# Building the expert gates inside the expert blocks: three PEER passes of a two-model forward on one core

## The chip, the cores and the metric

One core of a Trainium2 chip runs the whole program in one launch. The metric is the time of one execution in microseconds (us); lower is better.

## The reference, cut to what matters

A first block of mixers and a convolutional FFN is followed by two layers (l = 0, 1). Each layer ends in a PEER stage: every token picks, for each of 8 heads, 16 of 128 x 128 = 16384 experts, by the sums of two key scores, and the chosen experts act as a one-hidden-layer network.

```python
q      = rmsnorm(x) @ wq                    # [T, 8 heads x 128]
s1, s2 = q_half1 @ keys1.T, q_half2 @ keys2.T        # 128 scores each, per head
best 16 of (top16(s1)[:,None] + top16(s2)[None,:])   # row key, column key, softmax weight w
h      = gelu(x @ U[expert])                # for the chosen experts only
y      = sum over the chosen: w * h * V[expert]
```

The kernel computes it densely. It takes x @ U for all 16384 experts, multiplies by a gate that is zero wherever an expert was not chosen, and multiplies by all of V. The gate of a token is the 128 x 128 matrix sum_i w_i onehot(row_i) onehot(col_i)^T over its 128 chosen pairs, a matmul with the choice index on the contraction axis. There are T = 256 tokens a stream. Layer 0 does it for two streams (s = 0 and 1), layer 1 for one (s = 1): three passes.

## The kernel before, in words

Weights stream from HBM through `ring`, NS = 4 slots of 128 x 1024 float32 (512 KB). SyncE issues all their DMAs in one fixed order (`order`, function `stream`, L242): the transfer into a slot waits until the block that used the slot before is done (`blocks_done`). A product is made in three float32r parts: ScalarE writes the rounded high part into `ring_hi` (NH = 3 slots), another engine writes block minus high part over the ring slot (`ring_lo`), and TensorE multiplies hi x hi, hi x lo and lo x hi.

A PEER pass before the change, by lines:

- norm of the streams (`rms_phase`, L352 to L411), then queries in plain float32 (`product`, L1617) for both streams at once, evacuated by ScalarE (L1624), with a phase of their own;
- U (L1649 to L1861): TensorE first makes the key scores (L1691, all token tiles of both streams in pass one), ScalarE makes the high part of x (L1739), GpSimd its low part (L1667). Then 128 blocks c: ScalarE high part (L1745), GpSimd low part (L1673), TensorE 24 matmuls of 256 columns (L1706 to L1708) into banks 4 to 7, ScalarE gelu into S[:, c, :] (L1750). Beside it VectorE does the routing of 4 (pass one), 0 (pass two) or 2 tiles (pass three) (L1806 to L1859), and TensorE transposes its result (L1716);
- gate (L1871 to L1957), a phase of its own: 64 groups of 4 tokens. The one-hot columns come from GpSimd (L1885, 4 a group), the weighted one-hot rows half from VectorE (L1921), half from ScalarE (L1897, L1902). TensorE does 4 float32 matmuls of 128 columns a group (L1949; each has two rows in the trace), VectorE multiplies the bank into S (L1927);
- V (L1964 to L2040): 128 blocks. ScalarE high part of V (L1979); VectorE high and low part of the gate weights S[:, c, :] (L2001, L2003) and low part of V (L1994); TensorE 12 matmuls of 512 columns (L2027 to L2031) into banks 0 to 3;
- y is copied, transposed and added to X (L2053 to L2070).

Every phase ends in a barrier of all engines (L339). Loops are `Fori` of 12 blocks; within an engine the order is the written one, and every wait stands in that order.

Of the kernel before, what the change touches and what calls it, by code (L numbers as in the profile page):

```python
# [8 lines left out]
F32 = mybir.dt.float32  # L9
# [12 lines left out]
NS = 4  # L22
# [15 lines left out]
def small_columns():  # L38
# [123 lines left out]
def build(nc, x, smalls, consts, mix_tables, tables, axial, w_in1, w_lru, w_br, w_o1, w_f1, w_f2, ada, w_in2,  # L162
          w_out2, w_q2, keys2, peer_u, peer_v, out):
    ctx = ExitStack()
    with ctx:
# [12 lines left out]
        spill = nc.dram_tensor("spill", (P, KT, T), F32, kind="Internal").ap()  # L178
# [4 lines left out]
        n_arena = 36092  # L183
# [33 lines left out]
        for l in range(LAYERS):  # L217
            order += [(w_in2[l], i) for i in range(25)]
            order += [(w_out2[l], i) for i in range(8)]
            order += [(w_q2[l], i) for i in range(8)]  # L220
            for _ in range(2 if l == 0 else 1):
                order += [(peer_u[l], i) for i in range(NK)]
                order += [(peer_v[l], i) for i in range(NK)]
# [826 lines left out]
        for l in range(LAYERS):  # L1050
# [6 lines left out]
            gain1 = A.take(8, 2)  # L1057
            gain2 = A.take(8, 2)
# [4 lines left out]
            with Phase("v_chain", "v_lam", "a_lam") as (block, v_chain, v_lam, a_lam):  # L1063
                lam2 = A.take(2)
                prod = A.take(2, 64)

                @block.sync
                def _(sp):
                    stream(sp, 0)

# [6 lines left out]
                def _(dve):  # L1077
                    link = linker(dve, v_chain)
                    lp = sm(f"lam{l}").rearrange("p (a b c) -> p a b c", a=2, b=2)
                    link(dve.tensor_tensor(prod, lp[:, :, 0, :], lp[:, :, 1, :], ALU.mult))  # L1080
                    dve.tensor_reduce(lam2, prod, AX.X, ALU.add).then_inc(v_lam, 1)
                    for g, first, name in ((gain1, 8, "norm1"), (gain2, 32, "norm2")):
                        dve.scalar_tensor_tensor(g, mod[:, first:first + 8, :], 1.0,
# [7 lines left out]
            def norm_jobs(gain, first, ss):  # L1091
                return [((lambda kt, s=s: X[:, kt, s, :]), (lambda kt, s=s: H[:, kt, s, :]),
                         (lambda kt, s=s: gain[:, kt, s:s + 1]), (lambda kt, s=s: mod[:, first + kt, s:s + 1])) for s in ss]
# [4 lines left out]
            rms_phase(norm_jobs(gain1, 0, (0, 1)), lambda j, kt: (XH[:, kt, j, :], H_r[:, kt, j, :]))  # L1098
# [495 lines left out]
            rms_phase(norm_jobs(gain2, 24, streams))  # L1594


            R = [A.take(3, T) for _ in streams]
            peer_mark = A.at
            S = A.take(NK, T)
            extra = A.take(1700)  # L1600
            flat = S.rearrange("p c t -> p (c t)")
            qT = flat[:, 0:4096].rearrange("p (h t) -> p h t", h=PEER_H)
            KK = flat[:, 4096:5120].rearrange("p (h n) -> p h n", h=PEER_H)
            n0 = used[0]
            with Phase("by_act", "keys_in") as (block, by_act, keys_in):
                @block.sync
                def _(sp):
                    sp.dma_start(KK.rearrange("p a b -> p (a b)"), keys2[l]).then_inc(keys_in, 16)
                    stream(sp, 8)
                    sp.wait_ge(keys_in, 16)  # L1610

                @block.tensor
                def _(pe):
                    for b in range(8):
                        if b >= 4:
                            pe.wait_ge(by_act, b - 3)
                        product(pe, n0 + b, bank[b % 4][:, t0:],  # L1617
                                lambda kt: H[:, kt, t0 // T:, :].rearrange("p s t -> p (s t)"))

                @block.scalar  # L1620
                def _(act):
                    for b in range(8):
                        act.wait_ge(blocks_done, n0 + b + 1)
                        act.activation(qT[:, b, t0:], bank[b % 4][:, t0:], ACT.Copy).then_inc(by_act, 1)  # L1624
            used[0] += 8


            route = tiles
            first_row = 84
            SC = [flat[:, (first_row + 8 * n) * T:(first_row + 8 * n + 8) * T].rearrange("p (i k) -> p i k", k=NK)  # L1630
                  for n in range(4)]
            S2 = flat[:, 116 * T:124 * T].rearrange("p (i k) -> p i k", k=NK)
            cand2 = S2.rearrange("p i k -> p (i k)").rearrange("p (h k) -> p h k", k=256)
            tail = Space(flat[:, 124 * T:128 * T], 4 * T)
            best, bidx = tail.take(16, TOPK), tail.take(16, TOPK)
            bidx_u = tail.take(16, TOPK).bitcast(U32)
            pos_u = tail.take(PEER_H, TOPK).bitcast(U32)
            ext = Space(extra, 1700)
            top = [ext.take(PEER_H, TOPK) for _ in range(2)]
            found = [ext.take(3, PEER_H * TOPK) for _ in range(2)]  # L1640
            zsum = ext.take(2, PEER_H)
            half_u = ext.take(2, PEER_H, TOPK).bitcast(U32)
            half = ext.take(2, PEER_H, TOPK)

            for j, s in enumerate(streams):
                routing = route if j == 0 else []
                n0 = used[0]
# [551 lines left out]
```

## Time and profile before

| | |
|---|---|
| median of 3 runs | 4640.06 us (4624.87 to 4643.92) |
| profiled execution | 4631.07 us, of which the span is 4629.2 us, granted clock 0.905 |

```profile
## 1 busy us (share of the span) xinstructions
PE 4070.2 (88%) x23362; PEld 3457.1 (75%) x23362; DVE 1987.9 (43%) x4330; ACT 1820.1 (39%) x2910; POOL 1898.0 (41%) x1373
...
PE   7997789888677999789989997899786799987998
...
POOL 6830018041001988950018889300150088886000
PEclk9997899997678999779999996899995899987999
```

PE is TensorE's matmuls, PEld its weight loads, DVE VectorE, ACT ScalarE, POOL GpSimd. The lower lines are the span in 40 equal slices of 115.7 us, busy share or granted TensorE clock in tenths. The three passes lie in slices 12 to 20, 20 to 28 and 31 to 39 (counted from 0).

### The profile page before, as it was taken

How to read it: one execution, taken by the hardware profiler on the slowest of the kernel's cores; microseconds unless marked ns; L12 is line 12 of the kernel's file. 1: busy time of each engine (PE TensorE's matmuls, PEld its weight loads, DVE VectorE, ACT ScalarE, POOL GpSimd, SP SyncE). 2: the span in 40 equal slices, each digit the busy share in tenths (PEclk: the TensorE clock that was granted, in tenths of full speed). 3: DMA queues.
4: the chain of work that ended last, by engine and by line, in shares of the span. 5: the costliest groups of instructions: out<-in, count | busy, mean ns of one | idle time of the engine just before them, and what ended most of it. 6: DMA issues, size and time to landing. Idle time of an engine off the chain costs nothing. (4 is left out here: it accounts for less than half of the span.)

```text
span 4629.2 us, 69301 instructions
## 1 busy us (share of the span) xinstructions
PE 4070.2 (88%) x23362; PEld 3457.1 (75%) x23362; DVE 1987.9 (43%) x4330; ACT 1820.1 (39%) x2910; POOL 1898.0 (41%) x1373
## 2 busy tenths in 40 slices
PE   7997789888677999789989997899786799987998
PEld 7963479765434999768879996788674689976886
DVE  4013323163533972456650005666536290035665
ACT  4533014122213455653334556433432255565333
POOL 6830018041001988950018889300150088886000
PEclk9997899997678999779999996899995899987999
DMA  5575445321012555125545550255330245521554
GB/s 191 179 245 182 151 129 184 123 81 38 3 32 65 168 173 173 59 68 186 188 160 183 182 182 23 96 189 187 128 100 3 78 157 176 181 68 49 187 187 149
DMA packets 168892, 611.16 MB, mean 132 GB/s; under 512 B 18448, under 2 KB 21648, under 8 KB 168464
## 3 DMA queue, kind: packets, MB, share of 16 engines
q1 hardware_dynamic: 168720, 608.87, 40.0%
q8 instruction: 108, 1.77, 0.2%
q14 instruction: 64, 0.52, 0.0%
HBM read 606.70 MB, written 2.10 MB: 132 GB/s over the span
## 5 line engine op out<-in xcount | busy, mean ns | idle before, releaser
L1673 POOL TENSOR_TENSOR ring_r<-ring,ring_hi 128x1024 fp32r<-128x1024 f32 x384 | 970.8, 2535 | 187.2 <-ACT ring_hi L1745 186.2
L1706 PE MATMUL bank<-H_r,ring_hi 128*128 128x256 f32 x3072 | 876.0, 285 | 43.9 <-POOL ring_r L1673 43.9
L1707 PE MATMUL bank<-H_r,ring_hi 128*128 128x256 f32 x3072 | 871.8, 284 | 0.0
L1708 PE MATMUL bank<-H_r,ring_r 128*128 128x256 f32 x3072 | 871.7, 284 | 0.0
L278 POOL TENSOR_TENSOR ring_r<-ring,ring_hi 128x1024 fp32r<-128x1024 f32 x183 | 457.7, 2506 | 594.0 <-ACT ring_hi L272 593.5
L1979 ACT ACTIVATE ring_hi<-ring 128x1024 fp32r<-128x1024 f32 x384 | 407.3, 1062 | 689.4 <-DMA ring<-in_peer_v 648.9
L1706 PEld LDWEIGHTS bank<-H_r,ring_hi 128*128 128x128 f32 x3072 | 592.4, 193 | 50.8 <-issue 25.1
L1707 PEld LDWEIGHTS bank<-H_r,ring_hi 128*128 128x128 f32 x3072 | 592.4, 193 | 0.0
L1708 PEld LDWEIGHTS bank<-H_r,ring_r 128*128 128x128 f32 x3072 | 592.2, 193 | 0.0
L2027 PE MATMUL bank<-ring_hi,w_parts 128*128 128x512 f32 x1536 | 485.5, 397 | 10.3 <-DVE ring_r L1994 10.3
L2029 PE MATMUL bank<-ring_r,w_parts 128*128 128x512 f32 x1536 | 484.7, 397 | 0.0
L2031 PE MATMUL bank<-ring_hi,w_parts 128*128 128x512 f32 x1536 | 484.1, 396 | 0.0
L1994 DVE TENSOR_TENSOR ring_r<-ring,ring_hi 128x1024 fp32r<-128x1024 f32 x384 | 467.8, 1218 | 1.0 <-ACT ring_hi L1979 1.0
L1885 POOL TENSOR_SCALAR H<-CS,arena 128x128 f32<-128x128 f32 x768 | 446.1, 610 | 18.8 <-issue 18.8
L288 PE MATMUL bank<-H_r,ring_hi 128*128 128x256 f32 (+1 forms) x1464 | 452.1, 309 | 0.0
L1949 PE MATMUL bank<-H 128*128 128x128 f32 x1536 | 329.5, 382 | 129.3 <-DVE arena L1927 54.5
L1745 ACT ACTIVATE ring_hi<-ring 128x1024 fp32r<-128x1024 f32 x384 | 406.0, 1059 | 85.7 <-DMA ring<-in_peer_u 82.4
L1949 PEld LDWEIGHTS bank<-H 128*128 128x128 f32 x1536 | 285.3, 278 | 173.3 <-DVE arena L1927 81.8
L1667 POOL TENSOR_TENSOR H_r<-H,H_r 128x256 fp32r<-128x256 f32 x24 | 16.5, 727 | 968.8 <-ACT H_r L1739 968.8
L2027 PEld LDWEIGHTS bank<-ring_hi,w_parts 128*128 128x128 f32 x1536 | 289.1, 188 | 81.8 <-DVE ring_r L1994 11.1
L2029 PEld LDWEIGHTS bank<-ring_r,w_parts 128*128 128x128 f32 x1536 | 289.3, 188 | 71.0
L2031 PEld LDWEIGHTS bank<-ring_hi,w_parts 128*128 128x128 f32 x1536 | 289.2, 188 | 71.0
(319 smaller groups left out, 5946.7 us busy)
## 6 DMA issues: line engine op xcount, KB each, us to landing
ring<-in_peer_u SPq DMA_DIRECT2D x384, 512.0 KB, 3.4
ring<-in_peer_v SPq DMA_DIRECT2D x384, 512.0 KB, 3.4
ring<-in_w_in SPq DMA_DIRECT2D x135, 512.0 KB, 3.4
ring<-in_ada SPq DMA_DIRECT2D x96, 512.0 KB, 5.0
ring<-in_w_f SPq DMA_DIRECT2D x72, 512.0 KB, 3.5
ring<-in_w_br SPq DMA_DIRECT2D x24, 512.0 KB, 3.4
ring<-in_w_out SPq DMA_DIRECT2D x16, 512.0 KB, 3.5
ring<-in_w_q SPq DMA_DIRECT2D x16, 512.0 KB, 3.4
```

Source lines behind the costliest of these rows:

```text
L278: eng.tensor_tensor(ring_lo[:, slot, :], ring[:, slot, :], ring_hi[:, m % NH, :].bitcast(F32), ALU.subtract).then_inc(lows, 1)
L288: pe.matmul(o, hi[:, k], x_lo(kt), start=False, stop=False)
L1673: pool.tensor_tensor(ring_lo[:, slot, :], ring[:, slot, :], ring_hi[:, m % NH, :].bitcast(F32), ALU.subtract).then_inc(p_lo, 1)
L1706: pe.matmul(o, hi[:, k], x_hi_[:, kt, :], start=(kt == 0), stop=False)
L1707: pe.matmul(o, hi[:, k], x_lo_[:, kt, :], start=False, stop=False)
L1708: mm = pe.matmul(o, lo[:, k], x_hi_[:, kt, :], start=False, stop=(kt == KT - 1))
L1885: hot = pool.tensor_scalar(hotB[:, 4 * (g % 4) + u, :], cc("iota"), cols_[:, 4 * g + u:4 * g + u + 1], None, ALU.is_equal)
L1949: mm = pe.matmul(bank[q][:, u * P:(u + 1) * P], hotA[:, 4 * q + u, :], hotB[:, 4 * q + u, :], start=True, stop=True)
L1994: dve.tensor_tensor(ring_lo[:, slot, :], ring[:, slot, :], ring_hi[:, m % NH, :].bitcast(F32), ALU.subtract).then_inc(v_lo, 1)
L2027: pe.matmul(bank[2 * t + e][:, :], w_hi, hi[:, v], start=start, stop=False)
L2029: pe.matmul(bank[2 * t + e][:, :], w_hi, lo[:, v], start=False, stop=False)
L2031: mm = pe.matmul(bank[2 * t + e][:, :], w_lo, hi[:, v], start=False, stop=stop)
```

## The change

The two streams of layer 0 no longer share norm, queries and scores: for each stream one norm phase (which now also writes the float32r parts of x) and then **one single phase** holding queries, scores, U, gates and V. There is no barrier in it. The queries use the three-part product on the same ring, so w_q is streamed once for each pass. Copies to and from `spill` are gone. Gate groups are now of 8 tokens and 64 second keys (128 x 64 columns), 64 groups: groups 0 to 31 serve S[:, 0:64, :] and are built between U blocks 64 to 127, one for every two; groups 32 to 63 serve S[:, 64:128, :] and are built between V blocks 0 to 63. VectorE alone makes the one-hots, three instructions a group. In V the high part of the gate weights goes to ScalarE with four buffers (they lie in H), GpSimd has no work. The lambda table comes by a DMA of its own in each layer, not with the small tables.

```diff
-                        ("ln_g", 2), ("ln_b", 2), ("gate_b", 1), ("ml_norm", 1), ("df_norm", 1), ("lam", 256)):
+                        ("ln_g", 2), ("ln_b", 2), ("gate_b", 1), ("ml_norm", 1), ("df_norm", 1)):
...
+                    sp.dma_start(lamt, lam[l]).then_inc(lam_in, 16)
...
-            rms_phase(norm_jobs(gain2, 24, streams))
...
+            for s in streams:
+                A.at = 0
+                x_hi_, x_lo_ = H_r[:, :, 1 - s, :], H_r[:, :, s, :]
+                rms_phase(norm_jobs(32, 24, (s,)), lambda j, kt: (x_hi_[:, kt, :], x_lo_[:, kt, :]))
...
+                        with pool.Fori(0, 11) as it:
                             for m in range(12):
                                 low(m, it)
...
+                        def build(g, it=None):
+                            n = g if it is None else it * 6 + g
+                            pe.wait_ge(v_hot, n + 1)
+                            if it is not None or g not in (0, 1, 32, 33):
+                                pe.wait_ge(v_g, n - 1)
+                            o = bank[(0 if g < 32 else 4) + g % 2]
+                            for u in range(8):
+                                mm = pe.matmul(o[:, u * 64:(u + 1) * 64], hotA[:, g % 2, u, :], hotB[:, g % 2, u, :],
+                                               start=True, stop=True)
+                            mm.then_inc(g_ps, 1)
...
+                        for b in range(8):
+                            pe.wait_ge(p_lo, b + 1)
...
+                            parts_of(b, bank[4 + b % 4][:, 0:T])
+                        up(0)
...
+                        scores(0)
+                        up(1)
+                        up(2)
+                        pe.wait_ge(a_s, 4)
+                        scores(1)
+                        up(3)
...
+                        up_turns(0, 3)
+                        turn_found(0)
+                        up_turns(3, 4)
+                        turn_found(1)
+                        up_turns(4, 5)
...
+                        build(0)
+                        up(64)
+                        up(65)
+                        build(1)
+                        up(66)
+                        up(67)
+                        with pe.Fori(0, 5) as it:
+                            for i in range(6):
+                                build(2 + i, it)
+                                up(68 + 2 * i, it)
+                                up(69 + 2 * i, it)
+                        pe.wait_ge(a_gelu, NK)
+                        build(32)
+                        down(0)
+                        down(1)
+                        build(33)
+                        down(2)
+                        down(3)
+                        with pe.Fori(0, 5) as it:
+                            for i in range(6):
+                                build(34 + i, it)
+                                down(4 + 2 * i, it)
+                                down(5 + 2 * i, it)
...
+                        def weights(c, it=None):
+                            if it is not None or c >= 4:
+                                act.wait_ge(blocks_done, turns(it, n0 + v0 + c - 3))
...
+                            act.activation(W_hi[:, c % 4, :], w, ACT.Copy).then_inc(a_whi, 1)
...
+                        def hot(g, it=None):
+                            if g >= 2:
+                                dve.wait_ge(g_ps, g - 1 if it is None else it * 6 + (g - 1))
+                            dve.tensor_tensor(hotB[:, g % 2, :, :], second.unsqueeze(1).to_broadcast([P, 8, 64]),
+                                              cols_[:, bass.ds(t, 8)].unsqueeze(2).to_broadcast([P, 8, 64]),
+                                              ALU.is_equal).then_inc(v_col, 1)
+                            dve.tensor_tensor(hotA[:, g % 2, :, :], first.unsqueeze(1).to_broadcast([P, 8, P]),
+                                              rows_[:, bass.ds(t, 8)].unsqueeze(2).to_broadcast([P, 8, P]), ALU.is_equal)
+                            dve.wait_ge(v_col, g + 1 if it is None else it * 6 + (g + 1))
+                            dve.tensor_tensor(hotB[:, g % 2, :, :], hotB[:, g % 2, :, :],
+                                              wts[:, bass.ds(t, 8)].unsqueeze(2).to_broadcast([P, 8, 64]),
+                                              ALU.mult).then_inc(v_hot, 1)
+                        def gate(g, it=None):
+                            dve.wait_ge(g_ps, g + 1 if it is None else it * 6 + (g + 1))
...
+                            w = S[:, first:first + 64, bass.ds(t, 8)]
...
+                            dve.tensor_tensor(w, w, o, ALU.mult).then_inc(v_g, 1)
...
+                        with dve.Fori(0, 5) as it:
+                            for i in range(6):
+                                gate(i, it)
+                                hot(i + 2, it)
...
+                        with dve.Fori(0, 5) as it:
+                            for i in range(6):
+                                split(2 * i, it)
+                                low(2 * i, it)
+                                split(2 * i + 1, it)
+                                low(2 * i + 1, it)
+                                gate(32 + i, it)
+                                hot(34 + i, it)
```

GpSimd's loop makes the low parts of w_q and U, 136 blocks. Of VectorE's two loops the first stands beside U blocks 64 to 127, the second beside V blocks 0 to 63; `split` is now the low part of the gate weights alone and waits for ScalarE's high part (`weights`). After the interleaved half of V, `down` runs for blocks 64 to 127 without builds.

## Rows read from the trace of the kernel before

**Rows 1.** Windows: busy time (instructions) of PE, PEld, DVE, ACT, POOL; PEclk, DMA share, GB/s.

```profile
1389.00:1491.50 102.50, 75.01 (x288) 40.34 (x288) 26.18 (x126) 31.02 (x69) 7.93 (x10) 0.89 0.19 62
1491.50:1884.60 393.10, 377.28 (x3084) 373.09 (x3084) 233.27 (x725) 197.20 (x274) 335.99 (x127) 0.99 0.52 170
1884.60:2041.20 156.60, 109.86 (x512) 94.36 (x512) 88.43 (x198) 102.05 (x260) 148.79 (x256) 0.70 0.02 4
2041.20:2402.00 360.80, 360.76 (x1536) 289.36 (x1536) 235.34 (x381) 133.40 (x126) 0.00 (x0) 0.99 0.57 187
2402.00:2417.20 15.20, 3.59 (x16) 3.29 (x17) 3.44 (x8) 7.46 (x15) 7.94 (x10) 0.69 0.11 36
2417.20:2787.90 370.70, 370.67 (x3072) 370.48 (x3072) 0.00 (x0) 181.41 (x252) 304.83 (x127) 0.99 0.55 180
...
3652.30:3707.00 54.70, 39.03 (x209) 33.73 (x209) 13.57 (x67) 18.95 (x44) 8.04 (x10) 0.89 0.30 97
3707.00:4089.90 382.90, 374.24 (x3078) 371.82 (x3078) 115.06 (x359) 191.26 (x265) 322.58 (x127) 0.99 0.54 174
```

**Rows 2.** Groups of instructions: busy us, mean ns | idle before, releaser.

```profile
L1885 POOL TENSOR_SCALAR H<-CS,arena 128x128 f32<-128x128 f32 x768 | 446.1, 610 | 18.8 <-issue 18.8
...
L1927 DVE TENSOR_TENSOR arena<-arena,bank 128x512 f32 (+1 forms) x192 | 143.2, 746 | 199.0 <-PE bank L1949 198.2
```

**Rows 3.** Timelines of TensorE: start us, us of the merged rows, line, count.

```profile
2033.35 1.15 PE L1949 MATMUL bank<-H 128*128 128x128 f32 x8 [0.62 <-POOL H L1885]
...
297.92 1.05 PE L297 MATMUL bank<-CS,H 128*128 128x2 f32 x8
...
1122.09 8.79 PE L1334 MATMUL bank<-arena 128*128 128x65 f32 x40 [0.78 <-DVE arena L1396]
```

**Rows 4.** Timeline of TensorE where U blocks are parted by three transposes.

```profile
1604.73 0.49 PE L1716 MATMUL bank<-CS,arena 128*128 128x128 f32 x3
1604.98 0.36 PE L1706 MATMUL bank<-H_r,ring_hi 128*128 128x256 f32 x1
1605.18 0.28 PE L1707 MATMUL bank<-H_r,ring_hi 128*128 128x256 f32 x1
```

**Rows 5.** Groups of instructions that V keeps or moves, and gelu.

```profile
L1994 DVE TENSOR_TENSOR ring_r<-ring,ring_hi 128x1024 fp32r<-128x1024 f32 x384 | 467.8, 1218 | 1.0 <-ACT ring_hi L1979 1.0
...
L1979 ACT ACTIVATE ring_hi<-ring 128x1024 fp32r<-128x1024 f32 x384 | 407.3, 1062 | 689.4 <-DMA ring<-in_peer_v 648.9 <-PEq L339 27.3 <-PE bank L2031 13.3
...
L2003 DVE TENSOR_TENSOR w_parts<-arena,w_parts 128x256 fp32r<-128x256 f32 x384 | 163.5, 426 | 13.3 <-DVE w_parts L2001 0.2
...
L1750 ACT ACTIVATE arena<-bank 128x256 f32 (+1 forms) x384 | 148.5, 387 | 469.4 <-PE bank L1708 469.3
```

**Rows 6.** Timeline of VectorE in the routing, beside GpSimd's low parts.

```profile
1521.31 2.29 DVE L1856 TENSOR_TENSOR arena<-arena,CS 128x2048 f32<-128x2048 f32 x1
1523.63 4.37 DVE L1858 TENSOR_TENSOR arena<-arena 128x2048 f32<-128x2048 f32 x1
```

**Rows 7.** Timeline of GpSimd there: a low part alone, then seven in a run.

```profile
1518.72 2.40 POOL L1673 TENSOR_TENSOR ring_r<-ring,ring_hi 128x1024 fp32r<-128x1024 f32 x1 [0.41 <-ACT ring_hi L1745]
1521.69 24.42 POOL L1673 TENSOR_TENSOR ring_r<-ring,ring_hi 128x1024 fp32r<-128x1024 f32 x7 [0.57 <-ACT ring_hi L1745]
```

**Rows 8.** Timelines: end of a norm, low parts of one, the first scores.

```profile
3659.62 3.31 ACT L383 ACTIVATE H<-H,MODS 128x256 f32<-128x256 f32 x8 [2.34 <-DVE H L401]
...
3323.86 3.25 DVE L410 SCALAR_TENSOR_TENSOR H_r<-H,MODS,h_high 128x256 fp32r<-128x256 f32 x8
...
1464.36 2.06 PE L1691 MATMUL bank<-arena 64*128 64x128 f32 x32 [0.94 <-PEq L339]
```

**Rows 9.** DMA issues: count, KB each, median us from issue to landing.

```profile
ring<-in_peer_u SPq DMA_DIRECT2D x384, 512.0 KB, 3.4
...
CS<-in_consts SPq DMA_DIRECT2D x1, 137.0 KB, 2.2
```

**Rows 10.** Timelines: last step of pass one's y; first U block of the next, clock ramping.

```profile
2405.03 3.44 DVE L2070 SCALAR_TENSOR_TENSOR X<-bank,MODS,X 128x256 f32<-128x256 f32 x8 [6.72 <-PE bank L2063]
...
2417.57 0.41 PE L1707 MATMUL bank<-H_r,ring_hi 128*128 128x256 f32 x1
2421.97 0.28 PE L1706 MATMUL bank<-H_r,ring_hi 128*128 128x256 f32 x1
```

More of the change, by code:

```diff
@@ L1625, in build @@
[L1625 to L1635, printed above, removed]
@@ L1734, in _ @@
+                        for c in range(HALF + 60, NK):
+                            down(c)
                     @block.scalar
                     def _(act):
-                        if routing and not last:
-                            act.wait_ge(spilled, 16)
-                        for kt in range(KT):
-                            act.activation(x_hi_[:, kt, :], H[:, kt, s, :], ACT.Copy).then_inc(x_hi, 1)
                         def high(m, it=None):
@@ new lines, in _, with gelu_turns @@
+                        gelu(1)
+                        gelu(2)
+                        keep_scores(1)
+                        gelu(3)
+                        def gelu_turns(a, b):
+                            with act.Fori(a, b) as it:
+                                for c in range(4, 16):
+                                    gelu(c, it)
+                        gelu_turns(0, 2)
+                        softmax(0)
+                        gelu_turns(2, 3)
+                        softmax(1)
@@ new lines, in _ @@
+                        act.wait_ge(blocks_done, n0 + v0)
+                        act.wait_ge(v_g, 32)
+                        weights(0)
+                        weights(1)
+                        with act.Fori(0, 5) as it:
+                            for c in range(12):
+                                weights(2 + c, it)
+                                high(v0 + NH + c, it)
+                        for c in range(60, 62):
+                            weights(2 + c)
+                            high(v0 + NH + c)
@@ L1796, in _ @@
+                        act.wait_ge(v_g, 64)
+                        with act.Fori(0, 5) as it:
+                            for c in range(62, 74):
+                                weights(2 + c, it)
+                                high(v0 + NH + c, it)
+                        for c in range(122, 126):
+                            weights(2 + c)
                             if c + NH < NK:
-                                high(c + NH)
+                                high(v0 + NH + c)
                     @block.vector
@@ new lines, in _ @@
+                        for i in (30, 31):
+                            split(2 * i)
+                            low(2 * i)
+                            split(2 * i + 1)
+                            low(2 * i + 1)
+                            gate(32 + i)
+                        dve.wait_ge(v_g, 64)
+                        with dve.Fori(0, 5) as it:
+                            for i in range(12):
+                                split(HALF + i, it)
+                                low(HALF + i, it)
```

446 lines of the change are left out of this document (150 added, 296 removed).

## The prediction, made before the change was run

> **What bounds the kernel now.** I read the 40 slices first, then busy times by stage, then the groups of the gate, then timelines. In all three U stages and in V TensorE works back to back at a granted clock of 0.99: the U of pass two has 370.67 us of PE in 370.7 us, the V of pass one 360.76 in 360.8 [rows 1]. So a U block costs 370.7 / 128 = 2.90 us (24 matmuls, 0.120 us apart; 2.88 without the start), a V block 360.8 / 128 = 2.82 us. Three stretches are different. In the gate (156.6 us here, 156.3 in the other two passes, 469.2 in all) PE has 109.9 us at a clock of 0.70, while GpSimd is busy 148.8 [rows 1]: 4 one-hots of 0.610 us are 2.44 us a group of 4 tokens [rows 2], and 64 x 2.44 = 156. GpSimd bounds it. Before the first U 102.5 us go to norms, queries and scores of two streams, before the third 54.7, before the second only 15.2, since pass one has done its work [rows 1]. And the U of pass one is 22.4 us longer than that of pass two, of pass three 12.2 us longer; the difference is the routing on VectorE [rows 1].
>
> **The change part by part.**
>
> *Start of a pass.* New for each: norm, parts of x, first high and low part, queries. In pass three the norm runs from 3652.3 to the last L383 at 3662.9 [rows 1, 8], 10.6 us. The low parts of x add 3.3 us [rows 8]; they were 8 GpSimd subtractions before. Barrier 0.3 us, then one high part 1.06 [rows 5] and one low part 2.40 [rows 7]: 17.7 us. Queries are 8 blocks of 2.88 us plus about 2 us for the clock's ramp (rows 0.41 us long at first, 0.28 after 4 us) [rows 10]: 25. Total 42.7 us. Pass one: 102.5 becomes 42.7, -59.8. Pass three: 54.7 becomes 42.7, -12.0. Pass two: y ends at 2408.5 [rows 10], 6.5 us into its stretch, so 15.2 becomes 49.5: +34.3. Sum -37.5.
>
> *U and routing.* Every pass now routes 2 tiles, as pass three did in 382.9 us. Its ramp (2 us) has moved to the queries, two sets of scores move in (2.06 each [rows 8]), and I allow 2 us for ScalarE, which copies scores between two gelus while high parts wait behind it. 387 each: -6, +16, +4 against 393.1, 370.7, 382.9 [rows 1]. Sum +14. The routing ends some 140 us into U (pass three's took 132 us from its first scores), TensorE asks for it after block 52, some 160 us in: that wait is covered by 20 us.
>
> *The gates.* The three stages leave: -469.2. 64 groups of 8 matmuls go between the blocks, 16 rows of the trace each. What does a row cost? With 128 columns at full clock (1.15 - 0.27) / 7 = 0.126 us; with 2 columns (1.05 - 0.25) / 7 = 0.114; with 65 columns at half clock (8.79 - 0.42) / 39 = 0.215, that is 0.107 and a fixed part at full [rows 3]. So below 128 columns the weight load is what is paid, and 64 columns cost hardly less than 128. The halved columns with twice the matmuls double TensorE's gate work. I take 0.114: 1.82 us a group, and 0.08 us for changing between the kinds (0.20 instead of 0.12 us after the transposes [rows 4]): 1.90. 64 x 1.90 = 122 us a pass, all on the path, since TensorE bounds both stages. Bounds: 0.107 and 0.126, or 3 x 64 x 16 x (-0.007 to +0.012) = -22 to +37 us. From U to V: last gelu 0.39, high part queued before it 1.06, weights' high part 0.39 (like the gelu), low part 0.43, V's low part 1.22 [rows 5] are 3.5 us, of which build(32) fills 1.9. 1.6 us a pass. So 3 x 123.6 = 371: the gates give 469 - 371 = -98. V starts at full clock instead of ramping: -4.
>
> *VectorE beside U.* A group has three tensor_tensors over 512, 1024 and 512 elements. From 256 elements in 0.426 and 1024 in 1.218 us [rows 5]: 0.69 + 1.22 + 0.69 = 2.60 us, and 0.75 for the gate product [rows 2]. 3.35 us stand against a period of 2 x 2.88 + 1.90 = 7.66. But GpSimd is subtracting there. In the routing a product over 2048 elements took 2.29 us when it came just before a GpSimd subtraction and 4.37 when one was running; GpSimd's own went from 2.40 to 24.42 / 7 = 3.5 us in that run [rows 6, 7]. They take turns. Two subtractions and the three one-hot steps then need 4.81 + 2.60 = 7.41 us of 7.66, if they never idle. By hand through one period: group built at 0; gate product to 0.75; GpSimd, on the block freed before, to 2.0; VectorE 2.0 to 4.6; next subtraction (its high part ends 4.3) 4.6 to 7.0, the one after at 7.2. Both fit. A low part is used 3.5 us after it is made, the one-hots have 5 us of slack (two buffers). So I cost it at 0. Uncovered: VectorE's chain could be 4.81 + 2.60 + 0.75 = 8.16 us, +0.50 x 96 = +48 us; I keep that as the upper end. Here the Trainium skill, "SBUF — State Buffer", section "Who interferes with whom", speaks against the change: a VectorE instruction with two SBUF inputs and a GpSimd instruction that reads SBUF lock each other out for their whole length, whoever came first. The trace agrees (4.37 against 2.29 us). By the same section the gate product, with one input in PSUM, is free of it; by that rule alone the sum is the one above, and the rival below is its unlucky order.
>
> *VectorE and ScalarE beside V.* A period of two V blocks and a build is 2 x 2.82 + 1.90 = 7.54. VectorE: 2 x (0.43 + 1.22) + 0.75 + 2.60 = 6.65, with GpSimd still. Split and low of the next block stand behind gate and hot in its queue; they end 4.7 us after a build, and are wanted 7.5 after. ScalarE has 2 x (1.06 + 0.39) = 2.9. A ring transfer is issued at a block's end and lands 3.4 us later [rows 9]; three blocks (8.5 us) lie before its use, and high and low part take 2.3 to 3.5. Cost 0. If the cover goes, each us beyond 0.89 costs 96 us.
>
> *Lambda.* A DMA of 128 KB now stands before the first step of two short phases; 137 KB took 2.2 us [rows 9]. +5. Spill copies go; the one that was waited for is in pass one's 102.5.
>
> **Sum.** -37.5 + 14 - 98 - 4 + 5 = -120.5. The profiled execution's 4631.07 becomes 4510.6. That execution is 9 us under the median of the runs (4640.06) and above the lowest (4624.87). I put the time at 4515.
>
> **Rivals.**
> - *The turns fall badly in U.* For: 7.41 of 7.66 us are claimed, and the routing, with less of it, cost 12 us for 2 tiles. Against: the hand-made order fits. 4515 + 48 = 4563.
> - *Slower than before: VectorE becomes the bound.* The one-hot steps read broadcast operands; a group's have 2048 elements, as L1856 and L1858, which mostly took 4.37 us. If 4.37 is their own price and not a wait, V's group is 3.30 + 0.75 + 4.37 = 8.42 (+0.88 x 96 = 84 us) and U's 4.37 + 0.75 + 4.81 = 9.93 (+2.27 x 96 = 218). 4515 + 302 = 4817. It decides when VectorE's chain passes the period by 0.65 us a group on average (125 / 192), near 8.3 us. Against: the same instruction took 2.29 just before a subtraction.
> - *The clock.* If builds ran at half clock as most of the old gate stage did (0.70 granted, TensorE starved), rows cost 0.215: +0.10 x 3072 = +310, 4825. Against: transposes amid U left it at 0.99 [rows 1, 4].
> - *More than forecast.* ScalarE's 2 us and the routing's 12 could shrink, rows be 0.107: 4515 - 22 - 10 - 20 = 4463.
>
> **How the numbers follow.** Forecast 0.62 (own range 4490 to 4545), bad turns 0.20, VectorE 0.07, clock 0.04, more 0.07. The range 4470 to 4600 takes in the bounds and leaves out about 0.15. Half a per cent, 23 us, is about what can be told from no change. Faster 0.88, same 0.02, slower 0.10.
>
> **What would show it.** No stretch with PE under 0.9 busy between a pass's first query and its last V block; builds in runs of 16 rows of about 1.9 us at a clock of 0.99; one-hot steps of 0.7 to 1.2 us in V and sometimes 2 to 3 more in U. It is wrong if TensorE waits for one-hots or for GpSimd's low part before U blocks 64 to 127, or if PE's rows in a build are much over 0.12 us apart.

## The result, and the profile after

| | before | after |
|---|---|---|
| median of 4 runs each, taken together | 4638.53 us (4624.87 to 4643.92) | 4451.59 us (4450.95 to 4458.87) |
| profiled execution | 4631.07 us | 4458.87 us |
| its span, granted clock | 4629.2 us, 0.905 | 4457.1 us, 0.935 |

After / before is 0.9605, 95% interval 0.9582 to 0.9628: 187 us less. The forecast was 4515 with a range of 4470 to 4600. The direction and the mechanism held; the time lies 63 us below the forecast and 18 us below the range. The profiled executions differ by 172 us, not 187, because that of before is 8 us under its median and that of after 7 us over. The forecast's sum was -120.5 from one profiled execution, so -172 is what it is held against: 52 us are missing from it.

The page of after, busy times and 40 slices (111.4 us each):

```profile
PE 4037.1 (91%) x25218; PEld 3528.5 (79%) x25218; DVE 2383.2 (53%) x4156; ACT 1640.7 (37%) x2529; POOL 1527.5 (34%) x605
...
PE   7997698978858999999989999999796699999998
...
PEclk9997899989569999999999999999895799999999
```

The 7s in PE that stood for the three gate stages are gone. From slice 13 on TensorE's line is broken only between the passes: at the start of pass two (the 8 of slice 20) and at the second layer's mixers (slices 28 to 31). VectorE's share rose from 43 to 53%, GpSimd's fell from 41 to 34%.

Windows of after, columns as in [rows 1]; per pass the start (norm, or y and norm), from the first query to the first V, and V. Of pass one, queries, U and routing are parted from the U blocks with gates between, and of V the first half, with gates, is shown. The start of pass three, not shown, took 16.90 us:

```profile
1394.90:1412.10 17.20, 3.72 (x16) 2.96 (x16) 8.36 (x18) 9.28 (x20) 2.35 (x2) 0.73 0.21 61
1412.10:1637.40 225.30, 216.92 (x1798) 214.42 (x1799) 138.85 (x422) 112.36 (x159) 193.07 (x73) 0.99 0.55 166
1637.40:1878.30 240.90, 240.90 (x2050) 240.82 (x2048) 150.62 (x128) 88.75 (x128) 158.81 (x63) 1.00 0.46 140
1878.30:2107.40 229.10, 227.29 (x1259) 197.01 (x1257) 185.75 (x249) 86.33 (x128) 0.00 (x0) 1.00 0.46 143
...
2287.10:2311.70 24.60, 8.59 (x34) 6.26 (x33) 11.40 (x25) 12.63 (x25) 2.44 (x2) 0.71 0.14 45
2311.70:2777.90 466.20, 457.58 (x3840) 455.08 (x3841) 291.35 (x550) 201.30 (x287) 354.55 (x135) 0.99 0.49 152
2777.90:3190.90 413.00, 410.94 (x2057) 348.22 (x2055) 286.39 (x378) 173.28 (x255) 0.00 (x0) 0.99 0.53 164
```

The third row is the main reading of this case: 64 U blocks and 32 gate groups take 240.90 us, and PE is busy in all of it at a clock of 1.00. The period is 240.9 / 32 = 7.53 us. No one-hot and no low part made TensorE wait there. What this row replaces is a stage at 0.70 with PE busy 109.86 of 156.60 us [rows 1].

TensorE's timeline through one period of it, beside [rows 3, 4]:

```profile
1735.26 1.89 PE L1697 MATMUL bank<-arena 128*128 128x64 f32 x16
1736.96 0.36 PE L1659 MATMUL bank<-H_r,ring_hi 128*128 128x256 f32 x1
...
1742.78 1.89 PE L1697 MATMUL bank<-arena 128*128 128x64 f32 x16
```

Sixteen rows, 1.70 us from the build's first to the next block's first, which stands 0.20 us before its successor, as after the transposes of [rows 4], instead of 0.12. A build costs 1.70 + 0.08 = 1.78 us; the rows are (1.89 - 0.28) / 15, about 0.106 us, apart, since a lone matmul's row is some 0.28 long.

VectorE in the same period, then GpSimd, beside [rows 6, 7]:

```profile
1737.30 0.69 DVE L1941 TENSOR_TENSOR arena<-arena,bank 128x512 f32 x1 [2.81 <-PE bank L1697]
1737.90 2.67 DVE L1925 TENSOR_TENSOR arena<-CS,arena 128x512 f32<-128x512 f32 x1
1740.49 1.21 DVE L1928 TENSOR_TENSOR arena<-CS,arena 128x1024 f32<-128x1024 f32 x1
1741.63 0.68 DVE L1931 TENSOR_TENSOR arena<-arena 128x512 f32<-128x512 f32 x1
1744.82 0.69 DVE L1941 TENSOR_TENSOR arena<-arena,bank 128x512 f32 x1 [2.52 <-PE bank L1697]
```

```profile
1737.63 2.40 POOL L1644 TENSOR_TENSOR ring_r<-ring,ring_hi 128x1024 fp32r<-128x1024 f32 x1 [0.92 <-ACT ring_hi L1781]
1741.62 2.90 POOL L1644 TENSOR_TENSOR ring_r<-ring,ring_hi 128x1024 fp32r<-128x1024 f32 x1 [1.60 <-ACT ring_hi L1781]
```

The first one-hot step (L1925) began at 1737.90, while GpSimd's subtraction of 1737.63 ran until 1740.03; its record is 2.67 us long, where beside V the same step takes 0.68. GpSimd waits in turn: its record of 1741.62 is 2.90 us long instead of 2.40, and the last one-hot step (L1931), which began with it at 1741.63, kept its 0.68. They take turns as [rows 6] said, yet VectorE is still idle 2.5 to 2.8 us a group before the gate product.

The same engine beside V, where GpSimd does nothing:

```profile
1984.88 0.68 DVE L1925 TENSOR_TENSOR arena<-CS,arena 128x512 f32<-128x512 f32 x1
1985.48 1.22 DVE L1928 TENSOR_TENSOR arena<-CS,arena 128x1024 f32<-128x1024 f32 x1
...
1991.53 0.69 DVE L1941 TENSOR_TENSOR arena<-arena,bank 128x512 f32 x1 [1.29 <-PE bank L1697]
```

TensorE in V without builds, after, then the same place of before. Each row is two matmuls:

```profile
2199.96 0.62 PE L1711 MATMUL bank<-ring_hi,H_r 128*128 128x512 f32 x2
...
2201.77 0.61 PE L1713 MATMUL bank<-ring_r,H_r 128*128 128x512 f32 x2
```

```profile
2299.62 0.63 PE L2027 MATMUL bank<-ring_hi,w_parts 128*128 128x512 f32 x2
...
2301.49 0.63 PE L2029 MATMUL bank<-ring_r,w_parts 128*128 128x512 f32 x2
```

Both fences span 8 matmuls: 1.81 us after, 1.87 before. More exactly 0.2265 and 0.2333 us from start to start, over longer stretches. V's matmuls are the same in number, shape and type, at full clock in both, and nobody waits in either. In each, 128 columns of the gate weights' parts are loaded (the call is `pe.matmul(bank, w_hi, hi[:, v])`) and 512 columns of the block, in ring or ring_hi, are streamed. It is the loaded operand that the change touched: the parts lie in `w_parts` behind S before, in H after, with four buffers instead of two and the high part from ScalarE. This is what the forecast had not priced; the experiments part the place from the rest.

### The profile page after: what moved, and what is told of

The parts are those of the page before. It is cut to its first block and busy times, and to the rows that moved or that the text cites. A ratio compares the mean times of both kernels' runs of the same rounds, so it can differ in the third digit from the quotient of the medians.

```text
span 4457.1 us, 71091 instructions
## 1 busy us (share of the span) xinstructions
PE 4037.1 (91%) x25218; PEld 3528.5 (79%) x25218; DVE 2383.2 (53%) x4156; ACT 1640.7 (37%) x2529; POOL 1527.5 (34%) x605
## 5 line engine op out<-in xcount | busy, mean ns | idle before, releaser
L1659 PE MATMUL bank<-H_r,ring_hi 128*128 128x256 f32 x3264 | 938.4, 288 | 63.3 <-POOL ring_r L1644 60.3
L1660 PE MATMUL bank<-H_r,ring_hi 128*128 128x256 f32 x3264 | 926.0, 284 | 0.0
L1711 PE MATMUL bank<-ring_hi,H_r 128*128 128x512 f32 x1536 | 483.8, 396 | 4.5 <-DVE ring_r L1955 4.4
L1713 PE MATMUL bank<-ring_r,H_r 128*128 128x512 f32 x1536 | 474.6, 390 | 0.0
L1715 PE MATMUL bank<-ring_hi,H_r 128*128 128x512 f32 x1536 | 474.6, 390 | 0.0
L1955 DVE TENSOR_TENSOR ring_r<-ring,ring_hi 128x1024 fp32r<-128x1024 f32 x384 | 467.3, 1217 | 0.0
L1786 ACT ACTIVATE arena<-bank 128x256 f32 (+1 forms) x384 | 147.6, 384 | 666.3 <-PE bank L1661 666.0
L1697 PEld LDWEIGHTS bank<-arena 128*128 128x128 f32 x3072 | 365.5, 192 | 9.1 <-ACT arena L1786 2.0
L1697 PE MATMUL bank<-arena 128*128 128x64 f32 x3072 | 363.6, 271 | 1.4 <-ACT arena L1786 1.4
L1941 DVE TENSOR_TENSOR arena<-arena,bank 128x512 f32 x192 | 132.0, 687 | 430.3 <-PE bank L1697 430.3
L1925 DVE TENSOR_TENSOR arena<-CS,arena 128x512 f32<-128x512 f32 x192 | 307.1, 1599 | 86.9 <-ACT arena L1801 86.9
L1713 PEld LDWEIGHTS bank<-ring_r,H_r 128*128 128x128 f32 x1536 | 289.0, 188 | 61.3
L1715 PEld LDWEIGHTS bank<-ring_hi,H_r 128*128 128x128 f32 x1536 | 288.9, 188 | 61.2
L286 PE MATMUL bank<-H_r,ring_hi 128*128 128x256 f32 x1064 | 303.7, 285 | 28.5 <-POOL ring_r L277 28.5
```

The costliest lines, as they stand in the source:

```text
L1659: pe.matmul(o, hi[:, k], x_hi_[:, kt, :], start=(kt == 0), stop=False)
L1660: pe.matmul(o, hi[:, k], x_lo_[:, kt, :], start=False, stop=False)
L1697: mm = pe.matmul(o[:, u * 64:(u + 1) * 64], hotA[:, g % 2, u, :], hotB[:, g % 2, u, :], start=True, stop=True)
L1711: pe.matmul(bank[2 * t + e][:, :], w_hi, hi[:, v], start=start, stop=False)
L1713: pe.matmul(bank[2 * t + e][:, :], w_hi, lo[:, v], start=False, stop=False)
L1715: mm = pe.matmul(bank[2 * t + e][:, :], w_lo, hi[:, v], start=False, stop=stop)
```

## The experiments

All times are medians beside runs of the kernel before on the same chip (4635.16 to 4640.94 us). Where a kernel's ratio is given, it is to that. "Stride" is from the start of one matmul to the start of the next in V's second half.

### Why V became faster: place of the gate weights

Start addresses in a partition, from the allocations: ring 16512, ring_hi 32896, H 61568, each 128 above a multiple of 256. Before, `w_parts` was at 222048 and 218976, 96 above one. After, the parts are in H.

**e1_before_w64**, the kernel before with `w_parts` 32 bytes on (222080 and 219008, 128 above a multiple of 256):

```diff
-                at = (peer_mark + NK * T + 7) // 8 * 8
+                at = (peer_mark + NK * T + 15) // 16 * 16
```

> The kernel before, with one number changed: the tensor that holds the parts of the gate weights in V starts at a multiple of 64 bytes in its partition, where it started 32 bytes past one. It stays in the same region, and nothing else moves. Theory (the address of the weight operand sets the pace): a V matmul of 512 columns goes from 0.233 to 0.2265 us, start to start, V from 360.8 to about 350.4 us a pass, in all 3 x 1536 x 0.0068 = -31 us, ratio 0.993. Rival (the region, or who writes it): no change, V stays at 360.8 us and 0.233.

4610.96 us (4603.41 to 4616.14), ratio 0.9938 [0.9919, 0.9958]: 28 us less from an edit of one number. TensorE in V:

```profile
2299.43 0.62 PE L2031 MATMUL bank<-ring_hi,w_parts 128*128 128x512 f32 x2
...
2301.25 0.62 PE L2027 MATMUL bank<-ring_hi,w_parts 128*128 128x512 f32 x2
```

8 matmuls in 1.82 us, after's stride. That it lies in H doesn't matter; the start address does.

**e2_after_w32**, the kernel after with the parts 32 bytes on inside H:

```diff
-                W_hi, W_lo = (H_r[:, 2 * i:2 * i + 2, :, :]...
+                W_hi, W_lo = (h_flat[:, 1024 * i + 8:1024 * i + 1032]...
```

> The changed kernel, with the parts of the gate weights moved by 32 bytes inside the tensor H they lie in, so that they start 32 bytes past a multiple of 64 as they did before the change. Theory (address): V matmuls go back to 0.233 us, +31 us, from 4452 to about 4483, which would lie inside the predicted range. Rival (region, writer or four buffers): no change.

4487.05 us (4481.26 to 4497.84), ratio 0.9681 [0.9656, 0.9705], 35 us more than after:

```profile
2200.00 0.63 PE L1716 MATMUL bank<-ring_hi,H_r 128*128 128x512 f32 x2
...
2200.94 0.63 PE L1714 MATMUL bank<-ring_r,H_r 128*128 128x512 f32 x2
```

0.94 us for 4 matmuls here, 0.233 over longer stretches. So the effect can be put on and taken off in both kernels. With the old address the change would have come out at 4487, inside the range. How far do the addresses have to agree?

**e10_w_64on**, **e11_w_128on** and **e12_w_256on** are e2 with 64, 128 and 256 bytes (16, 32, 64 elements in place of 8).

> The changed kernel with the parts of the gate weights moved on by 64 bytes inside H, where moving them by 32 bytes cost 35 us. Theory (what counts is the start within 64 bytes): no change, 4452, V matmuls 0.2265 us apart. Rival (it must be a multiple of 128 bytes, as it is in the changed kernel and was in the first experiment): again about 4487 and 0.233 us.

> The changed kernel with the parts of the gate weights moved on by 128 bytes inside H; 32 and 64 bytes each cost about 35 us. Theory (a weight operand that starts at a multiple of 128 bytes is taken up faster): no change, 4452, V matmuls 0.2265 us apart. Rival (only this one place in H, or a larger multiple such as 256 bytes, is fast): about 4487 and 0.233 us.

> The changed kernel with the parts of the gate weights moved on by 256 bytes inside H; 32, 64 and 128 bytes each cost 31 to 37 us. In every fast kernel so far they start 128 bytes past a multiple of 256, as the ring slots do. Theory (the start within 256 bytes counts): fast again, 4452, V matmuls 0.2265 us apart. Rival (any place but the start of H is slow, or a larger multiple counts): about 4485 and 0.233 us.

4488.52 (4483.58 to 4493.85), 4482.75 (4480.42 to 4491.12) and 4459.75 us (4453.46 to 4460.15). Strides 0.233, 0.2325 and 0.2265. TensorE in V of e12:

```profile
2199.55 0.62 PE L1716 MATMUL bank<-ring_hi,H_r 128*128 128x512 f32 x2
...
2201.36 0.62 PE L1712 MATMUL bank<-ring_hi,H_r 128*128 128x512 f32 x2
```

The theories that a start on 64 or on 128 bytes is enough fell; 256 bytes on, the fast stride is back. All slow cases so far differ from the ring as well as from one fixed residue. Which of the two is it?

**e13_all_128on**, the kernel after with 128 bytes of nothing ahead of the ring, so that ring, ring_hi and parts all move together:

```diff
+        sb("pad", [P, 32])
```

> The changed kernel with 128 unused bytes ahead of the ring, so that ring, high parts, x, gate weights and arena all start 128 bytes later, and their distances stay. Theory A (the weight operand and the streamed operand must start alike within 256 bytes; only the difference counts): no change, 4452. Theory B (an operand must itself start 128 bytes past a multiple of 256): V goes to 0.233 us a matmul, about 4485, and U and queries, whose weights and streams lie in the ring and in H too, may slow as well, by up to 0.0068 x 9792 = 67 us more, 4550.

4454.66 us (4450.79 to 4463.53), ratio 0.9608 [0.9591, 0.9625], stride 0.2265:

```profile
2199.67 0.61 PE L1714 MATMUL bank<-ring_r,H_r 128*128 128x512 f32 x2
...
2201.49 0.62 PE L1716 MATMUL bank<-ring_hi,H_r 128*128 128x512 f32 x2
```

The parts now start on a multiple of 256 and e11's did too: there the stride was 0.2325, here 0.2265. What counts in V is the difference between the starts of the loaded operand (parts) and the streamed one (ring), within 256 bytes. Equal is fast (e12's 256 bytes are equal in this sense); 32 below, and 32, 64 and 128 above are slow.

**e3_after_xh64** applied it in another place, the mixers' high part of x in front of the two layers, before e10 to e13 were known: its start moves from 82656 to 82688, from 224 to 0 in 256.

```diff
-            A.at = (A.at + 7) // 8 * 8
+            A.at = (A.at + 15) // 16 * 16
```

> The changed kernel, with the high part of x in the second model's input projection (h_high) moved from 32 bytes past a multiple of 64 to a multiple of 64. There it is the streamed operand of two in three matmuls of 512 columns, at 0.233 us. If the address of a streamed operand counts as that of a weight operand: 0.2265 us there, 1200 matmuls, -8 us or 0.2%. If only the weight operand's address counts: no change.

4452.64 us (4449.69 to 4457.22), ratio 0.9602 [0.9579, 0.9624]: no change in time. Here the high part of x is the streamed operand and the ring the loaded one. The stride went from 0.2333 to 0.2283, while the waits for GpSimd's low parts in that stretch grew from 43.0 to 46.1 us, which took it back. By e13 the place tried was not the right one (0 against the ring's 128). Yet the stride fell by 2% as the difference went from 96 to 128 bytes, and a difference of 128 had cost V its full 0.006 us (e11). So the difference alone does not give the size of the loss; what else sets it was not separated, and the rule above is shown for V.

### What bounds TensorE's turns beside U

**e4_half_builds**: only 4 of the 8 matmuls of each build are done, the rest of the gates left out.

```diff
-                            for u in range(8):
+                            for u in range(4):
```

> The changed kernel, leaving out half of the gate matmuls (4 of the 8 in each of the 64 groups a pass); all waits, one-hots and gate products stay. Theory (TensorE sets the pace beside U and V and each matmul costs two rows of 0.106 us whatever its columns): a group loses 0.85 us; V, where VectorE needs 6.5 of then 6.3 us, gains most of 0.85 x 96 = 82 us, U the same if GpSimd and VectorE can take turns in less than 6.7 us, or only up to 7.4 us (some 10 us in all) if the shared turns, 4.8 + 2.6 us, are the next bound. So 4370 to 4290 by the first, about 4365 by the second. Rival (something else sets the pace there already): no change.

4311.23 us (4300.37 to 4312.91), ratio 0.9295 [0.9275, 0.9316]: 140 us less than after. A build's first row to the next block's is 0.81 us instead of 1.70; 192 x 0.89 = 171 us were to be had, and 140 came. So TensorE was the bound of both stages. Beside V's first half nearly every group takes 6.37 us, from build to build, instead of 7.26. Beside U most groups take 6.63 us, all of 0.89 less than after's 7.53, but twice in every pass a group takes some 8.5 us, and mostly the next one 8.2. Here the build before began at 1695.90:

```profile
1704.35 1.10 PE L1697 MATMUL bank<-arena 128*128 128x64 f32 x8 [1.65 <-DVE arena L1931]
1712.59 1.00 PE L1697 MATMUL bank<-arena 128*128 128x64 f32 x8
```

TensorE waits 1.65 us for one-hots, and the granted clock behind that wait is 0.75 from 1704 to 1708 us, so that the next group takes 8.24 us as well. Why it has to wait is in this window of e4 beside U and in VectorE's timeline there:

```profile
1640.00:1820.00 180.00, 176.52 (x1462) 176.11 (x1462) 180.00 (x106) 72.57 (x105) 146.49 (x53) 0.98 0.49 152
```

```profile
1735.52 2.29 DVE L1925 TENSOR_TENSOR arena<-CS,arena 128x512 f32<-128x512 f32 x1
1737.73 1.21 DVE L1928 TENSOR_TENSOR arena<-CS,arena 128x1024 f32<-128x1024 f32 x1
1738.87 2.86 DVE L1931 TENSOR_TENSOR arena<-arena 128x512 f32<-128x512 f32 x1
...
1742.25 2.29 DVE L1925 TENSOR_TENSOR arena<-CS,arena 128x512 f32<-128x512 f32 x1
```

VectorE's records now touch, with two of a group's four steps stretched by turns with GpSimd. A group takes 1742.25 - 1735.52 = 6.73 us here, 0.1 us more than TensorE's 6.63, and VectorE is busy in all 180 us of the window: it falls behind by that much a group until TensorE waits. 6.73 us is the bound that the turns set, 0.8 us below the period of after.

**e8_spare_step**: the kernel after with one comparison of 512 elements more in each group, written to a spare bank.

```diff
+                            dve.tensor_tensor(spare, second.unsqueeze(1).to_broadcast([P, 8, 64]),
+                                              rows_[:, bass.ds(t, 8)].unsqueeze(2).to_broadcast([P, 8, 64]), ALU.is_equal)
```

> The changed kernel with one step more on VectorE in each gate group: a fourth comparison over 512 elements with two SBUF inputs, written to a bank that nobody reads (0.69 us). Theory (VectorE's chain hides while it is shorter than TensorE's period, 7.5 us beside U and 7.2 beside V): beside V 6.4 + 0.7 = 7.1 us, hidden; beside U the turns of VectorE and GpSimd need 7.0 + 0.7 = 7.7 us, 0.2 to 0.5 us too many: +20 to +48 us, about 4485. Rival (VectorE is already the bound): +0.69 x 192 = +132 us. Rival (much room): 0.

4456.52 us (4450.18 to 4465.07), ratio 0.9622 [0.9606, 0.9638]: 5 us more than after, of the 20 or more expected, and within the spread of the runs. VectorE beside U:

```profile
1740.97 2.85 DVE L1934 TENSOR_TENSOR arena<-arena 128x512 f32<-128x512 f32 x1
...
1747.71 0.69 DVE L1931 TENSOR_TENSOR bank<-CS,arena 128x512 f32<-128x512 f32 x1
1748.32 2.87 DVE L1934 TENSOR_TENSOR arena<-arena 128x512 f32<-128x512 f32 x1
```

From one L1934 to the next are 7.35 us without a gap, and TensorE's period stayed at 7.53 us. The chain is all but full and costs nothing. My expectation added the new step to the old stretches; the idle time took it up, and the waits moved from one step to another.

**e6_weights_dve**: the high part of the gate weights back on VectorE.

```diff
-                            act.activation(W_hi[:, c % 4, :], w, ACT.Copy).then_inc(a_whi, 1)
...
+                            dve.tensor_copy(W_hi[:, c % 4, :], w).then_inc(a_whi, 1)
```

> The changed kernel with one part undone: the high part of the gate weights is made by VectorE again (a copy of 256 columns, 0.29 us), not by ScalarE; still four buffers in H. Theory (TensorE sets V's pace, VectorE has room): VectorE needs 6.4 + 0.6 = 7.0 us a period of 7.2 us beside V's first half and 1.9 of 2.7 us a block in the second: no change, 4452 within 10 us. Rival (VectorE's order is tight there): up to +0.6 x 96 = 58 us.

4449.27 us (4447.24 to 4457.22), ratio 0.9604 [0.9588, 0.962]: no difference. That part of the change is worth nothing here; TensorE hides it either way.

### What a build costs

**e9_16_columns**: the gate matmuls stream 16 columns instead of 64; three quarters of the gates are left out.

```diff
-                                mm = pe.matmul(o[:, u * 64:(u + 1) * 64], hotA[...], hotB[:, g % 2, u, :],
+                                mm = pe.matmul(o[:, u * 64:u * 64 + 16], hotA[...], hotB[:, g % 2, u, 0:16],
```

> The changed kernel with each gate matmul streaming 16 columns in place of 64, leaving out the gates of three quarters of the second keys; number of matmuls, waits and VectorE's steps stay. Theory (below some hundred columns TensorE pays for the weight load only): rows stay 0.106 us apart, a group 1.78 us, no change, 4452 within 10 us. Rival (the columns are paid): two passes of 48 columns fewer are 0.04 us a matmul, 0.32 us a group, -61 us, about 4390.

4458.22 us (4456.47 to 4461.57), ratio 0.9611 [0.9593, 0.9629]. TensorE of e9 beside U:

```profile
1741.84 1.85 PE L1697 MATMUL bank<-arena 128*128 128x16 f32 x16
1743.54 0.36 PE L1659 MATMUL bank<-H_r,ring_hi 128*128 128x256 f32 x1
```

Again 1.70 us: the columns are free, a row costs 0.106 us with 16 or 64.

**e7_gates_r**: both one-hot tiles are float32r, so that each gate matmul is one row, not two. The softmax weights are rounded to that format, nothing is left out.

```diff
-                hotA = A.take(2, 8, P)
-                hotB = A.take(2, 8, NK // 2)
+                hotA = nc.alloc_sbuf_tensor_at(f"hotA{l}{s}", [P, 2, 8, P], F32R, offset=hot_at)
+                hotB = nc.alloc_sbuf_tensor_at(f"hotB{l}{s}", [P, 2, 8, NK // 2], F32R, offset=hot_at + 8 * 8 * P)
```

> The changed kernel with the one-hot tiles as float32r: the one-hot rows stay exact, the softmax weights are rounded to float32r, and a gate matmul is one pass through TensorE instead of two. Theory (TensorE pays by weight loads): a group falls from 1.78 us to about 0.9 us, as when half of the matmuls were left out, which gave 4311; the same here, 4300 to 4320, V giving about 82 us and U only some 58, where VectorE and GpSimd in turns need about 7.0 us a group. Rival (a short single-pass matmul costs the 0.12 us of a 256-column one): 8 x 0.12 = 0.96 us, about 4325.

4310.26 us (4303.27 to 4312.47), ratio 0.9297 [0.9281, 0.9312], 141 us less than after: the version that beats both kernels. TensorE beside U:

```profile
1738.11 0.98 PE L1699 MATMUL bank<-hotB,hotA 128*128 128x64 f32 x8
1738.91 0.36 PE L1661 MATMUL bank<-H_r,ring_hi 128*128 128x256 f32 x1
```

0.80 us a build, 192 x 0.90 = 173 us to be had. It ends where e4 ends, 4311, and in the same way: beside U its groups take 6.64 us, and twice a pass TensorE waits for the one-hots of VectorE, which takes turns with GpSimd there.

### Whether the interleaving is the gain

**e5_gates_apart**: the same builds and one-hots, but all U blocks first, then 64 groups, then all V blocks.

```diff
                         build(0)
-                        up(64)
-                        up(65)
                         build(1)
-                        up(66)
-                        up(67)
```

> The changed kernel with the gates taken out from between the blocks: all 128 U blocks, then all 64 gate groups, then all 128 V blocks, within the same single phase, same one-hots, same matmuls, same four buffers. Theory (the gain of the gates comes from filling VectorE's and GpSimd's idle time beside U and V): a group is then bound by VectorE alone, 0.69 + 0.69 + 1.21 + 0.68 = 3.2 us with GpSimd idle, 64 x 3.2 = 205 us a pass, and 64 x 1.78 = 114 us of TensorE leave the blocks: 3 x (205 - 114) = +273 us, about 4725, slower than the kernel before. Rival (the gain comes from the new form of the groups and the missing barriers): within 50 us of 4452.

4775.74 us (4765.72 to 4777.09), ratio 1.0305 [1.0288, 1.0322]: 324 us more than after, and slower than before. The window of its gate stage, then one stretch of VectorE in it:

```profile
1811.00:2030.50 219.50, 217.03 (x1026) 215.87 (x1024) 188.12 (x249) 1.44 (x2) 0.00 (x0) 0.52 0.01 3
```

```profile
1829.82 0.69 DVE L1922 TENSOR_TENSOR arena<-arena,bank 128x512 f32 x1 [0.46 <-PE bank L1697]
...
1833.26 0.69 DVE L1922 TENSOR_TENSOR arena<-arena,bank 128x512 f32 x1 [0.41 <-PE bank L1697]
```

The granted clock is 0.52, the 1.2 GHz level, and PE is busy in 217.03 of 219.50 us. A group takes 1833.26 - 1829.82 = 3.44 us, 16 rows of 0.215 us, twice what the same rows take between U blocks at 1.00. VectorE waits for TensorE by 0.4 us a group, where I had expected VectorE's own 3.2 us to be the bound and 4725 us.

At the start of the stage it was as I had expected:

```profile
1810.97 3.68 PE L1697 MATMUL bank<-arena 128*128 128x64 f32 x32
1816.17 1.99 PE L1697 MATMUL bank<-arena 128*128 128x64 f32 x16 [1.53 <-DVE arena L1912]
```

The first two groups ran back to back at full clock, 32 rows in 3.68 us; then TensorE waited for one-hots, 1.53 and 0.94 us. With these waits the clock fell (0.84 from 1816 to 1820 us, 0.50 from there on), a group's rows took longer than VectorE's steps, and the waits were gone. So the 324 us are the half clock as the kernel ran: 192 x (3.44 - 1.78) = 319 us. Had it stayed full, VectorE's chain of about 3.03 us (1829.82 to 1832.84) would have been the bound: an estimate of 192 x (3.03 - 1.78) = 240 us.

## Why the prediction was wrong

**The starts of the passes: right.** 17.2 and 16.9 us from norm to first query in passes one and three against 17.7; 24.6 from V's last block in pass two against 6.5 + 0.3 + 17.7.

**The routing, the transition and U: right within 2 us a pass.** From the first query to the first V matmul it took 470.1, 471.1 and 470.9 us; the terms gave 25 + 387 + 33 builds of 1.90 + 1.6, about 476. Of the 5 to 6 us 4 are the builds' price, next.

**The builds: the mechanism right, the term mis-sized.** 1.78 us, not 1.90. The forecast took the 0.114 us row of 2 columns [rows 3] as the nearest; the row was 0.106, at the low end that I had kept (0.107 from 65 columns at half clock). 192 x 0.12 = 23 us. e9 shows that 16 columns cost the same as 64, so it isn't the columns; why the 2-column rows are dearer wasn't tried. The rival "more than forecast" (4463) had this way of being wrong: of its terms the row's 22 us came, the 10 and 20 us of ScalarE and the routing did not.

**The step that failed: V's block kept at 2.82 us.** The change put the gate weights in a new place ("they lie in H"), and the prediction gave that no term, neither a value nor bounds: its period beside V is 2 x 2.82 + 1.90. The blocks took 12 x 0.2265 = 2.72 us. The difference of 0.0068 us over 3 x 1536 = 4608 matmuls is 31 us. The runs put it at 28 (e1, in the kernel before) and 35 (e2, in the kernel after). Together with the builds that is 54 us. The stretches of the three passes sum to 2688.5 us against 2869.7 before, 181 us less where the forecast had 125.5 (its 120.5 and the 5 for lambda, which stand outside): 56 us are missing there, and 54 of them are these two. Outside the passes after's execution is 9 us longer where the forecast had 5, which gives the 52. Without V's 31 the builds alone would have left the time at 4483, within the range (e2 measured 4487): the range was too narrow by just the edit that had no bound.

**VectorE beside U at no cost: right.** PE 240.90 of 240.90 us. The rival "bad turns" claimed 8.16 us a group; e8, with one step more than that, runs in 7.35. Two things in the rows shorten the rival's sum: a step's record is 0.68 us long, but the next one starts 0.60 us after it (1984.88, 1985.48), and the gate product, short at 0.69, runs while GpSimd subtracts. They don't account for all of it. e4 puts the turns' own bound near 6.7 us (6.9 with its waits), so the cover was 0.6 to 0.8 us a group, more than the 0.25 of the prediction's working. The Trainium skill, "SBUF — State Buffer", section "Who interferes with whom", has the two lock each other out for the whole instruction; the stretched steps (2.67 against 0.68 us) and GpSimd's 2.90 against 2.40 agree, and so does the gate product from a bank, which stayed at 0.69.

**The rival VectorE as a bound: false.** The one-hot steps took 0.68, 1.22 and 0.68 us beside V, the sizes the forecast had read from [rows 5]; the broadcast costs nothing (1.22 us for 1024 elements with it and, in L1955, without). By that the 4.37 us of [rows 6] were waiting, though that step was not run without GpSimd.

**The rival of the clock: false in the change, true in its absence.** Amid U blocks the builds ran at 1.00; alone (e5) at 0.52, row 0.215 us, as the rival said. So the interleaving earns twice: the builds run at full clock, and by e5's first groups they would wait for one-hots without it, even at full clock.

**Beside V: right.** 0.68 + 1.22 + 0.68 + 0.69 + 2 x (0.42 + 1.22) is 6.55 us by its records, with 1.29 us idle a group in after. e6 finds the weights' high part free on either engine.

## What to carry to other kernels

Where a change moves a tile that TensorE streams, or one it loads, its start address is part of the price: here equal starts within 256 bytes of both gave 3% more pace to V's back-to-back float32r matmuls of 512 columns, for one number in an allocation. Neither the reach of this to other shapes nor its reason is shown, so it is to be tried in each place. Short float32 matmuls were priced by their rows here, not by their columns (16 or 64), and they belong between long ones that keep the clock up; to halve their rows (float32r) was worth as much as leaving out half of them. When the bound engine is covered by others by half a microsecond a group, an experiment that halves its work tells at once where the next bound lies.

## What the runs showed of the hardware

- TensorE's stride for V's float32r matmuls of 128 x 128 by 512 is 0.2265 us when loaded and streamed operand start at the same place within 256 bytes, and 0.2325 to 0.2335 us when they differ by 32, 64 or 128 (e1, e2, e10 to e13). Moved together they stay fast. The Trainium skill, "SBUF — State Buffer", section "Who interferes with whom", gives TensorE two independent read ports, for the loaded and the streamed operand, and has it wait for no one; that no other engine holds it up fits these runs, yet the stride depends on where its own two operands lie. In the mixers, with the ring loaded instead of streamed, a difference of 128 bytes in two of three matmuls gave 0.2283 (e3). What in the chip does it, and what other differences and shapes give, stays open.
- Rows of float32 matmuls of 16 and of 64 columns are 0.106 us apart at full clock, 1.70 us for 8 matmuls; as float32r 0.80 us for 8.
- With nothing but such float32 matmuls, 99% busy by their records for 219.5 us, the granted clock was 0.52 (e5); between blocks of 256-column matmuls, 1.00. It had fallen with two waits of TensorE (1.53 and 0.94 us) and did not come back while the rows ran without a gap. Busy in the trace and full clock are not the same thing. Why it stays low there wasn't settled.
- VectorE and GpSimd in turns: 7.35 us of VectorE's records a group stood against a period of 7.53 with no cost in time (e8).
